# Two projection tiles moved from the Fourier stage into the first scan group, with attention's parted split, tile order and scan waits rearranged

## The reference, cut to what matters

```python
def even_mixer(...):                      # layer 0
    fl, zl, xbcl, dtl = split(ul @ w_in)  # Fourier, gate, conv input, step sizes
    xs, b, c, dt = ssd_inputs(...)        # silu(depthwise conv of 5 taps), softplus
    y = bidir_ssd(xs, b, c, dt, a, ...)   # 4 groups, chunks of 128 tokens, both directions
    return concat([fourier_mix(fl), ssd_output(y, xs, zl, d_skip, norm_g)]) @ w_out
def odd_mixer(...):                       # layer 1
    qw, kw, vw, qn, kn, vn = split(u @ w_in)     # q and k are RMS-normalised, window's rotated
    ol = concat([window_attention(...), neighbourhood_attention(...)]) @ w_out
```

## Time and profile before

| | |
|---|---|
| median of 3 runs | 1428.59 us (1428.32 to 1431.62) |
| the profiled execution, its own time | 1428.98 us |
| its span | 1427.2 us |
| busy over the span | PE 1298.1 us (91%), weight loads 1024.9 (72%), DVE 787.1 (55%), ACT 503.3 (35%), POOL 88.9 (6%) |
| DMA | 166.68 MB, mean 117 GB/s |
| mean granted PE clock | 0.943 of full |

### The profile page before, as it was taken

How to read it: one execution, slowest core, us unless ns; L and a number is a source line. 1 busy time by engine, 2 the same in 40 slices (tenths; PEclk the granted TensorE clock), 3 DMA queues, 4 the chain that set the end, 5 groups by cost and what they waited for, 6 DMA issues and landing times.

```text
span 1427.2 us, 18737 instructions
## 1 busy us (share of the span) xinstructions
PE 1298.1 (91%) x7212; PEld 1024.9 (72%) x7212; DVE 787.1 (55%) x1235; ACT 503.3 (35%) x862; POOL 88.9 (6%) x72
## 2 busy tenths in 40 slices
PE   4799987898998899999999999999789778899998
PEld 1566765677776677767777777777677446899998
DVE  2643485577686535364343353443677564667764
ACT  2422043353543522152122222121633454534442
POOL 0000010100101000400000000004020000300000
PEclk8799998899998999989999999999899988999999
DMA  9454110111111012434444354443332101455553
GB/s 385 201 237 162 45 45 15 45 45 59 45 47 43 31 59 83 161 104 141 169 154 152 122 175 154 154 152 113 110 110 83 37 1 36 140 180 180 187 177 132
DMA packets 41531, 166.68 MB, mean 117 GB/s; under 512 B 4481, under 2 KB 6657, under 8 KB 38401
## 3 DMA queue, kind: packets, MB, share of 16 engines
q1 hardware_dynamic: 41040, 164.58, 33.0%
q10 hardware_dynamic: 432, 1.32, 0.2%
HBM read 164.83 MB, written 1.05 MB: 116 GB/s over the span
## 4 chain that ended last, share of the span: by engine, by line
PE 76%; issue 8%; DVE 8%; ACT 5%; DMA 3%; SPq 0%; POOL 0%; DVEq 0%; ACTq 0%; POOLq 0%
PE ps L1498 52%; PE ps L1505 8%; PE ps L1520 3%; PE ps L1719 2%; PE ps L1721 1%; DMA mring<-in_w_mod 1%; PE ps L1659 1%; PE ps L1839 1%; PE ps L1693 1%; PE ps L1678 1%; DVE sm L1450 1%; ACT ey L980 1%; PE ps L1853 1%; PE ps L1830 1%; ACT u L892 1%
## 5 line engine op out<-in xcount | busy, mean ns | idle before, releaser
L1498 PE MATMUL ps<-a_hi,w_hi 128*128 128x512 f32 (+1 forms) x880 | 332.3, 378 | 5.5 <-DVE w_lo L1087 5.5
L1498 PE MATMUL ps<-a_lo,w_hi 128*128 128x512 f32 (+1 forms) x880 | 317.9, 361 | 0.0
L1498 PE MATMUL ps<-a_hi,w_lo 128*128 128x512 f32 (+1 forms) x880 | 317.6, 361 | 0.0
L842 ACT ACTIVATE w_hi<-raw 128x1024 fp32r<-128x1024 f32 x206 | 217.0, 1055 | 273.8 <-DMA raw<-in_w_ff 205.8
L1087 DVE TENSOR_TENSOR w_lo<-raw,w_hi 128x1024 fp32r<-128x1024 f32 x206 | 256.9, 1248 | 78.2 <-ACT w_hi L842 77.6
L1498 PEld LDWEIGHTS ps<-a_hi,w_hi 128*128 128x128 f32 x880 | 170.7, 194 | 46.2 <-issue 13.8
L1498 PE MATMUL ps<-b_hi,w_hi 128*128 128x512 f32 (+1 forms) x560 | 193.8, 346 | 0.0
L1498 PE MATMUL ps<-b_hi,w_lo 128*128 128x512 f32 (+1 forms) x560 | 192.0, 343 | 0.0
L1498 PE MATMUL ps<-b_lo,w_hi 128*128 128x512 f32 (+1 forms) x560 | 191.3, 342 | 0.0
L1498 PEld LDWEIGHTS ps<-a_lo,w_hi 128*128 128x128 f32 x880 | 170.8, 194 | 26.4 <-issue 1.9
L1498 PEld LDWEIGHTS ps<-a_hi,w_lo 128*128 128x128 f32 x880 | 170.1, 193 | 25.3
(11 more groups left out here) (217 smaller groups left out, 1482.1 us busy)
## 6 DMA issues: line engine op xcount, KB each, us to landing
raw<-in_w_ff SPq DMA_DIRECT2D x128, 512.0 KB, 3.3
mring<-in_w_mod SPq DMA_DIRECT2D x24, 1024.0 KB, 7.9
mring<-in_w_mod SPq DMA_DIRECT2D x32, 768.0 KB, 5.0
raw<-in_w_in_even SPq DMA_DIRECT2D x36, 512.0 KB, 3.3
raw<-in_w_in_odd SPq DMA_DIRECT2D x18, 512.0 KB, 3.3
raw<-in_w_out_even SPq DMA_DIRECT2D x16, 512.0 KB, 3.3
raw<-in_w_out_odd SPq DMA_DIRECT2D x8, 512.0 KB, 3.5
bias<-in_rpb_na SPq DMA_DIRECT2D x8, 256.0 KB, 4.1
```

The costliest lines, as they stand in the source:

```text
L842: nc.scalar.activation(w_hi[:, u % RING, :, :], raw[:, u % RING, :, :], ACT.Copy).then_inc(hi_done, 1)
L1498: ins = mm(out_ap, w_[:, n % RING, k, :], x_[:, k, 0:ntok], start=(k == 0 and j == 0), stop=(k == KT - 1 and j == 2))
```

## The change

- Conv tiles 13 and 17 leave the Fourier stage and take slots 0 and 1 of group 0, so no slot of group 0 is empty. The 16 `mu` products are spread anew (`MOD_WITH`).
- `toks` of the next group stand before and after the last z tile, ahead of `ygate`. ACT does the `btok` copy. POOL's `xw` waits only for its own chunk. `ysum` of the group before moves ahead of the states. `cb` is one DVE instruction instead of two. `y` waits for `ycomb` only after its first twelve products.
- Group 3: the z tiles take slots 0 to 2, slot 3 is empty, and `mixsplit` 0 moves ahead, right behind the first `y`.
- The weights of `outB` 1 are prepared ahead of `mixsplit` 1 (`early`). A pair waits for its second tile's `w_lo` only at the second slice.
- The 18 tiles of layer 1 are interleaved so that v tiles stand between q and k tiles. The column mask is built into the bias table on the host, and POOL's addition is gone.
- Attention: `osplit` is parted. ACT's half (`ohi`) stands right behind `S`, DVE's half (`olo`) behind `scale`. ACT takes one small exponential before the first pass.

```diff
+MOD_WITH = (0, 1, 2, 4, 5, 7, 9, 11, 13, 14)
+       for kind, i in (q.split(".") for q in ("qw.0 qw.1 v.0 qw.2 qw.3 v.1 kw.0 v.2 qn.0 qn.1 v.3 qn.2 qn.3 kn.0 kn.1 kn.2 kn.3 v.4").split())]
...
-        for g, k in rest[2 * n:2 * n + 2]:
+        for g, k in rest[MOD_WITH[n]:MOD_WITH[n + 1]]:
             mods(g, k)
         s.extend(dft.get(n, []))
-    gemm("conv", conv_tiles(1)[0])
-    s += [("dfts", 2), ("dftw", 3)]
-    gemm("conv", conv_tiles(1)[1])
-    s.append(("dfts", 3))
+    for g, k in rest[MOD_WITH[9]:]:
+        mods(g, k)
...
+    s += [("dfts", 2), ("dftw", 3), ("dfts", 3)]
...
-            convs = [("conv", t) for t in conv_tiles(g + 1)[2 * (g == 0):]]
+            convs = [("conv", t) for t in conv_tiles(g + 1)]
...
-            slots = [None] + zs + [("outA", m) for m in range(4)]
+            slots = zs + [None] + [("outA", m) for m in range(4)]
...
+            if g == G - 1 and n == 0:
+                s.append(("mixsplit", 0))
...
         if g < G - 1:
+            s += [("toks", g + 1, c_) for c_ in ch[:2]]
             slot(7)
+            s += [("toks", g + 1, c_) for c_ in ch[2:]]
         s.append(("ygate", g))
...
-        for kind, i in (("S", j + 2), ("max", j + 1), ("scale", j), ("exp", j + 1), ("PT", j), ("osplit", j - 2), ("O", j - 1)):
+        for kind, i in (("S", j + 2), ("ohi", j - 2), ("max", j + 1), ("scale", j), ("olo", j - 2), ("exp", j + 1), ("PT", j), ("O", j - 1)):
...
+        early = ("gemm", "outA", KT - 1)
...
-                elif st == ("dup",):
-                    pool.wait_ge(bias_in, 16 * 8)
...
-                        pool.tensor_tensor(bias[:, qt, :, :], bias[:, qt, :, :], cuts["nam"][:, None, :].broadcast_to([P, 8, SEQ]),
-                                           ALU.add).then_inc(bias_done, 1)
...
-                    pool.wait_ge(xdt_done, tok_n[("toks", g, SCAN_F[-1])] + 1)
+                    pool.wait_ge(xdt_done, tok_n[("toks", g, ch)] + 1)
...
+                    nc.scalar.activation(btok[:, ch, :], ps[:, b, GX:GX + NS], ACT.Copy).then_inc(signal(btok_done), 1)
...
-                    v.tensor_tensor(cbm[:, 0, :], ps[:, b, 0:P], tle, ALU.mult).then_inc(signal(dve_seq), 1)
-                    v.tensor_tensor(cbm[:, 1, :], ps[:, b, 0:P], tge, ALU.mult).then_inc(freeing(st), 1)
+                    v.tensor_tensor(cbm[:, :, :], ps[:, b, None, 0:P].broadcast_to([P, 2, P]), masks, ALU.mult).then_inc(freeing(st), 1)
...
                     pe.wait_ge(g_done, 2 * n + 2)
-                    pe.wait_ge(y_done, n + 1)
...
+                    pe.wait_ge(y_done, n + 1)
+                    for i in range(XT):
                         ins = mm(ps[:, b, P * i:P * i + P], ycomb[:, n % 2, P * i:P * i + P], ident, start=False, stop=True, skip_group_check=True)
```

More of the change, by code:

```diff
@@ L216, in script @@
         ch = SCAN_F
-        for c_ in ch:
-            s.append(("toks", g, c_))
+        if g == 0:
+            s += [("toks", g, c_) for c_ in ch]
         s += [("cb", g, ch[0]), ("seg", g, "f", ch[0])]
         slot(0)
+        if g:
+            s.append(("ysum", g - 1))
         states(0)
         s.append(("seg", g, "b", ch[0]))
-        if g:
-            s.append(("ysum", g - 1))
         states(2)
@@ L260, in script @@
     s += [("norm", 0, "ff"), ("mlp", 0), ("norm", 1, "mix")]
-    for n, (kind, i, _, _) in enumerate(ODD):
-        gemm(kind, i)
+    for n in range(len(ODD) + 3):
+        if n < len(ODD):
+            gemm(*ODD[n][:2])
         for back, stage in ((1, "hstat"), (2, "hnorm"), (3, "rot")):
-            if n >= back:
+            if 0 <= n - back < len(ODD):
                 o = ODD[n - back][:2]
@@ L927, in _ @@
                 elif k == "gemm":
-                    high(unit[st] + AHEAD)
+                    if st != early:
+                        high(unit[st] + AHEAD)
                     b, _ = jobs[st]
@@ L1002, in _ @@
                     hi = (a_hi, b_hi)[st[1]]
+                    if st[1]:
+                        high(unit[early] + AHEAD)
                     for last_read in readers(st):
@@ L1206, in _ @@
                 elif k == "gemm":
-                    low(unit[st] + AHEAD)
+                    if st != early:
+                        low(unit[st] + AHEAD)
                     b, _ = jobs[st]
@@ L1357, in _ @@
                     hi, lo = ((a_hi, a_lo), (b_hi, b_lo))[st[1]]
+                    if st[1]:
+                        low(unit[early] + AHEAD)
                     for f in range(KT):
@@ L1510, in pair_product @@
                     first = part(0, k)
-                    if k == 1 and second_free:
-                        pe.wait_ge(*second_free)
+                    if k == 1:
+                        for q in second_waits:
+                            pe.wait_ge(*q)
                     if k:
@@ L1625, in _ @@
                         pe.wait_ge(*emptied(st))
[L1626 removed]
+                    pe.wait_ge(lo_done, unit[st] + 1)
                     ends = pair_product([ps[:, jobs[q][0], 0:tokens(q)] for q in pair], [unit[q] for q in pair], hi, lo, tokens(st),
[L1628 removed]
+                                        (split_done, starts[st] + 1),
+                                        [(lo_done, unit[pair[1]] + 1)] + ([emptied(pair[1])] if free_before[pair[1]] else []))
                     for q, ins in zip(pair, ends):
@@ L1899, in neighbour_bias @@
     c = np.clip(cols[None, :] - cols[:, None] + 15, 0, 30)
-    a = np.asarray(rpb)[0][:, r, c]
+    first = np.clip(cols - 8, 0, GRID_W - 16)[:, None]
+    inside = (cols[None, :] >= first) & (cols[None, :] < first + 16)
+    a = np.where(inside, np.asarray(rpb)[0][:, r, c], np.float32(NEG))
     return a.reshape(8, 2, P, SEQ).transpose(2, 1, 0, 3)
```

70 lines of the change are left out of this document (34 added, 36 removed).

## The result

| | before | after |
|---|---|---|
| median | 1428.45 us (1428.29 to 1431.62) | 1376.54 us (1376.19 to 1377.91) |
| span of the profiled execution | 1427.2 us | 1376.1 us |
| mean granted PE clock | 0.943 | 0.961 |

The ratio is 0.9633, 95% interval 0.9617 to 0.965: 51.9 us faster. The forecast was 1376 us.

The account below looks back on a forecast made before the run. PE, busy 91% of the span, was taken as the bound, with time won only where it idles or runs at its lower clock. Gains of 11.3, 15.6, 1.7, 5.8 and 18.6 sum to 53.0: 1428.98 to 1376 us, range 1358 to 1394.

Parts of the forecast that it names:

- Attention (18.6): Attention passes: with the split parted, DVE no longer waits for ACT's a_hi; 18.6 us won, between 13 and 21.
- Part 1: Fourier stage and group 0: moved tiles fill empty slots ahead of y; 11.3 us won, between 7 and 14.
- Part 2: Three changes of group: toks moved ahead win 18.3 us, ysum ahead of states costs 2.7; 15.6 won, 9 to 19.
- Its own sign of failure: In the scan groups: the prediction is wrong if the states wait more than 3 us for the square root.
- Part 3: Group 3, with outA, outB and MLP pairs: empty slot moved, mixsplit 0 early; 1.7 us won, between -4 and 7.
- The hole: Group 3, before outA's pair: 5.6 us idle replaces today's 5.57 us wait, more work at lower clock; 1.7 us lost.
- The MLP pairs' 0.8: MLP pairs of tiles: 0.8 us won, counted within group 3's 1.7.
- Part 4: Layer 1's 18 tiles: POOL's additions go, v tiles between give DVE time; 5.8 us won, between 2 and 9.
- the waits that the prediction listed: New tile order of layer 1: 0.5 us for rot, 3.5 in dup, 6.0 at the end for kn 3's tail.
- The rival that rested on it (1380): Table switches at group changes cost the page's 2.66 us, 1.4 more per group: 1380 us, chance 0.05.

Follow-up runs that it names:

- e3: Changed kernel with conv tiles 13 and 17 back between the last Fourier transforms, slots 3 and 4 of group 0 empty again: 1380.3 us, ratio 0.9663.
- e6: Kernel before with y's twelve products first, then the three additions, and the wait for ycomb behind the products: 1411.9 us, ratio 0.9882.
- e5: Kernel before with y's twelve products first, then the three additions, the wait for ycomb still ahead of them: 1418.6 us, ratio 0.9932.
- e2: Changed kernel with ysum of groups 0 and 1 back behind the first two states and seg b: 1369.8 us, ratio 0.9600.
- e8: Changed kernel with toks of groups 1 to 3 back at the start of their group, behind ygate: 1383.5 us, ratio 0.9709.
- e10: Changed kernel with ysum as in e2, last yt one step earlier, second dup in its own bank, one more v tile behind kn 3: 1361.1 us, ratio 0.9524.
- e11: e10 with, in groups 1 and 2, the previous group's ygate behind the first conv tile, ysum the second, yrow and ynorm the third: 1354.6 us, ratio 0.9489.
- e7: Changed kernel with layer 1's 18 tiles in the old order, the mask still built on the host: 1371.3 us, ratio 0.9605.
- e12: Kernel before with three edits together, attention's split parted, the mask built on the host, y exactly as changed: 1384.7 us, ratio 0.9691.

## Why the total was right and the parts were not

**Attention (18.6) and its mechanism: right.** 18.5 in the change, 20.4 alone.

**Part 1 (11.3): the total of the stage hides a wrong step.** The prediction took the waits ahead of `y` and the low clock around them as won by the tiles that fill the slots. e3 shows the tiles worth 4.8, below the lower bound of 7; e6, without them, wins 8.9 of the stage's 16.0. The late wait for `ycomb` closes most of the same holes by itself. The prediction gave that edit 1.7 us, once, for the last `y`. It measured 6.7. No run isolates the 2.3 us that are left of the stage, the new spread of the `mu` products among them.

**The term left out.** No step of the prediction costs the new order in `y`. It was read as the frame of the late wait, not as an edit. It is worth 10.0 us (e5), the largest part of the change after the split. Rows of `y` before and after differ by 0.7 us where nothing waits; looking at how one step is spaced would have raised the question, though no row of before priced the other order.

**Part 2 (15.6, 9 to 19): wrong, and two prices failed, that of the moved `toks` (6.1 us won at each change) and that of `ysum` ahead of the states (0.9 lost).** Two groups won 1.2 us, less than the 4.1 that `y` alone gives there (e6). From the second z tile of group 0 to that of group 2:

| `toks` | `ysum` | kernel | us |
|---|---|---|---|
| behind `ygate` | behind the states | e6 | 169.8 |
| ahead | behind seg b | e2 | 170.1 |
| behind `ygate` | ahead | e8 | 176.8 |
| ahead | ahead | changed | 172.7 |

All four have the new `y`; e6 alone lacks the change's smaller edits and the two moved tiles. So `toks` ahead won nothing measurable where `ysum` stays back and some 2 us a group where it doesn't, and `ysum` ahead costs 1.3 us a group, 3.5 where `toks` stay behind `ygate`. The prediction counted `toks` from PE's side, as a wait that goes. PE's wait for `xdt` did go (8.1 us in these two groups of e6), and 9.8 us of others stand in its place in e2: 3.7 for the second `toks`' bank, which `yt` frees behind `gate`, and 6.1 for `hent` ahead of `ysum`, because DVE's `ygate` and ACT's square now stand ahead of `ey`. Both were then taken away, and the two groups fell by 6.7 us (e10) and 4.5 more (e11). For `ysum` the prediction bounded ACT's queue and forgot what hangs behind it: seg b on PE, its product on DVE, the taps, `hent`, `cb`. That is 1.5 for the root and some 3 more for `hent` in each group, of which some 3 come back ahead of `ysum` when it stands behind seg b. Its own sign of failure, "wrong if the states wait more than 3 us for the square root", stayed silent: the wait showed up two steps later, under another name.

**Part 3 (1.7, -4 to 7): too low.** The hole is near the forecast, 4.52 us and 0.26 for 5.6. Wrong was the clock behind it: outA's pair runs at the upper level (granted 1.00, before 0.86), 11.38 us against 12.88. The outB pair's second half waits 2.51 us, so 1.0 of the 3.5 is won (0.9 forecast). From the second z tile of group 2 to the norm 13.3 us were won; 4.3 of them come with `y` (e6) and 2.3 to 2.8 with `toks` (e8), which leaves 6.2 to 6.7 to group 3's order, the pairs and the clock. The MLP pairs' 0.8 didn't come: the stage lost 1.8, of which 1.2 stands between the start of the norm's statistics and the MLP's pair, where the granted clock is 0.55 and was 0.71. No experiment isolates group 3's order from its `ysum`, or the pairs from either.

**Part 4 (5.8, 2 to 9): size right, reason half.** POOL's additions were the whole gain, 6.6 us alone. The interleaving, credited with giving DVE time, costs about 2 (e7) through the waits that the prediction listed: 2.46 in dup (3.5 forecast), 5.02 ahead of the first `S` (6.0):

```profile
1085.94 3.35 DVE L1349 RECIPROCAL nt<-nt 128x512 f32<-128x512 f32 x1 [1.21 <-ACT nt L1002]
1089.21 1.31 DVE L1425 SCALAR_TENSOR_TENSOR kT<-kT,vec,nt 128x512 f32<-128x512 f32 x2
```

It lies with nothing over it, since `hstat` stands behind the next tile. One more v tile covers it (e10). The prediction's sum for the stage is 0.8 us too good by its own terms: ten tiles of 5.7 and six of 3.1 are 75.6, not 75.2, and 1023.6, 83.4, 0.5, 3.5 and 6.0 make 1117.0, not 1116.6.

**The table load.** Between the load at 262.07 (1.28 us) and the next activation at 263.36 there is no gap. The Trainium skill, "ScalarE: Activation LUTs", section "What ACT_TABLE_LOAD costs", adds a drain of 1.38 us; this trace doesn't show one. The rival that rested on it (1380) fell. The loads are as many as before, two a group; in groups 1 and 2 both now stand ahead of the second seg's product, where the kernel before had the second one later, at 293.76.

**How the errors met.** Forecast and not had: 9.2 in two changes of group, 1.2 in part 4, 0.7 at the end, 1.8 in MLP 0. Had and not forecast: 4.7 before group 1, 6.4 from group 2's second z tile on. Both of the latter contain `y`, whose 16.7 us make up for `ysum` and `toks`. That the total fits within 1 us is luck: a gain that was not foreseen stands against a loss of the same size. Three small edits, the split, `y` and the mask, give 44 of the 52 us (e12). The rearrangement that the change is named for gives the other 8, among them edits that cost.

## What to carry to other kernels

List every edit in the diff, also one that only swaps a loop, and give it a price and bounds before summing; then an error of 10 us can't hide behind a total. When a step moves past others in a fixed list, follow the queues of all engines until the first step that nobody waits for: the cost of `ysum` went from PE through ACT and DVE and came back to PE a tile later, as a wait for `hent`; and the wait for `xdt` that `toks` got rid of came back for work that DVE and ACT still had to do first. And try each half of a rearrangement alone: undoing the half that cost and covering what was left bare gave another 22 us.

## What the runs showed of the hardware

Alternating on PE between 128x64 products and 128x128 additions into one PSUM bank costs time, with nothing waited for. Twelve products, then three additions, take 2.23 us (e5); four and one, three times, take 2.92 (before): about 0.17 us for each of the four further switches. Whether it is the change of tile shape, the addition following at once on the products that it adds to, or the start flag, which is set less often in the new order, was not tried.
